# Scaling attention probabilities on VectorE, regrouping the gated unit, and splitting late norm chunks from PSUM

## The reference

```
# gated unit: D_FF = 2816 = 22 chunks of 128
up = hn @ w_up
gate = gelu(causal_dwconv(up[..., :D_FF], conv_f_w, conv_f_b))      # 3 taps
h = h + (gate * up[..., D_FF:]) @ w_down
# three norms whose result feeds the next product: cross attention, gated unit, final
y = x * rsqrt(mean(x * x) + 1e-6) * g
# NSA: the selected and the window branch, per head
p = masked_softmax(q k^T)            # here both branches see every earlier token
o = g0 * o_cmp + g1 * (p_sel @ v_sel) + g2 * (p_win @ v_win)        # g: sigmoid gates
```

## Time and profile before

| | us |
|---|---|
| median of 3 runs | 1995.47 |
| lowest, highest | 1994.6, 1995.6 |
| profiled execution, its time | 1993.29 |
| profiled execution, its span | 1991.5 |

### The profile page before, as it was taken

One profiled execution on the slowest core, in us unless ns is written; L12 is line 12 of the kernel. 1 busy time (PEld: TensorE's weight loads), 2 busy tenths in 40 slices (PEclk: granted clock), 3 DMA queues, 4 the chain that ended last, 5 costly groups with the idle time before them and its releaser, 6 DMA issues.

```text
span 1991.5 us, 24447 instructions
## 1 busy us (share of the span) xinstructions
PE 1903.8 (96%) x8906; PEld 1518.8 (76%) x8906; DVE 798.9 (40%) x1245; ACT 422.5 (21%) x827; POOL 1147.5 (58%) x686
## 2 busy tenths in 40 slices
PE   7989999999999999988989999998999989999996
PEld 5868787888888877865778888887765768888885
DVE  4965443453341464646451212126243362112126
ACT  4323312210010020145140101013233231101022
POOL 5635662675666675467546655664642446666652
PEclk9989999999999999989999999999999999999999
DMA  5312331232333335200223332332321123333321
GB/s 221 111 56 83 97 105 42 85 106 85 112 99 95 95 96 201 64 22 1 75 65 104 95 95 84 95 104 70 102 74 32 53 74 96 105 105 96 98 91 43
DMA packets 46879, 175.99 MB, mean 88 GB/s; under 512 B 5200, under 2 KB 5328, under 8 KB 46032
## 3 DMA queue, kind: packets, MB, share of 16 engines
q1 hardware_dynamic: 46512, 169.55, 26.9%
q10 hardware_dynamic: 288, 5.31, 0.7%
HBM read 172.74 MB, written 2.10 MB: 88 GB/s over the span
## 4 chain that ended last, share of the span: by engine, by line
PE 91%; DVE 3%; POOL 3%; issue 1%; ACT 1%; DMA 0%; SPq 0%; POOLq 0%; DVEq 0%; ACTq 0%
PE acc L466 16%; PE acc L468 16%; PE acc L467 16%; PE acc L489 8%; PE acc L490 7%; PE acc L493 7%; POOL p_n L2329 2%; PE acc L1015 1%; PE misc L1048 1%; PE acc L514 1%; PE acc L516 1%; PE acc L515 1%; PE acc L1017 1%; PE acc L1016 1%; PE misc L730 1%
## 5 line engine op out<-in xcount | busy, mean ns | idle before, releaser
L2316 POOL TENSOR_SCALAR w_hi<-raw 128x1024 fp32r<-128x1024 f32 x309 | 336.2, 1088 | 759.3 <-PE acc L493 381.3
L2318 POOL TENSOR_TENSOR w_lo<-raw,w_hi 128x1024 fp32r<-128x1024 f32 x309 | 746.5, 2416 | 25.8
L466 PE MATMUL acc<-x_hi,w_hi 128*128 128x512 f32 x872 | 342.9, 393 | 0.0
L468 PE MATMUL acc<-x_hi,w_lo 128*128 128x512 f32 x872 | 339.6, 389 | 0.0
L467 PE MATMUL acc<-x_lo,w_hi 128*128 128x512 f32 x872 | 339.4, 389 | 0.0
L466 PE MATMUL acc<-y_hi,w_hi 128*128 128x512 f32 x590 | 231.1, 392 | 0.0
L468 PE MATMUL acc<-y_hi,w_lo 128*128 128x512 f32 x590 | 229.6, 389 | 0.0
L467 PE MATMUL acc<-y_lo,w_hi 128*128 128x512 f32 x590 | 229.6, 389 | 0.0
L1718 DVE TENSOR_TENSOR h<-acc,h 128x512 f32<-128x512 f32 x120 | 82.8, 690 | 349.5 <-PE acc L468 215.8
L468 PEld LDWEIGHTS acc<-x_hi,w_lo 128*128 128x128 f32 x872 | 163.7, 188 | 34.1
L466 PEld LDWEIGHTS acc<-x_hi,w_hi 128*128 128x128 f32 x872 | 163.9, 188 | 32.9 <-issue 0.3
(11 more groups left out here) (374 smaller groups left out, 2657.9 us busy)
## 6 DMA issues: line engine op xcount, KB each, us to landing
raw<-weights_dram SPq DMA_DIRECT2D x309, 512.0 KB, 3.5
w_cmp<-w_cmp_dram ACTq DMA_DIRECT2D x1, 4096.0 KB, 15.9
h<-x_dram SPq DMA_DIRECT2D x2, 1024.0 KB, 6.1
out_dram<-h SPq DMA_DIRECT2D x8, 256.0 KB, 2.0
small<-small_dram SPq DMA_DIRECT2D x1, 1408.0 KB, 16.0
small<-small_dram ACTq DMA_DIRECT2D x1, 1088.0 KB, 6.3
mem_in<-mem_dram SPq DMA_DIRECT2D x1, 1024.0 KB, 13.0
const<-const_dram SPq DMA_DIRECT2D x1, 640.0 KB, 9.0
```

The lines of the kernel that those rows point to most:

```text
L466: mm(out, m["w_hi"][:, slot, k], hi[:, k], start=k == 0, stop=False)
L468: last = mm(out, m["w_lo"][:, slot, k], hi[:, k], start=False, stop=k == kc - 1)
L2316: nc.gpsimd.tensor_scalar(hi, m["raw"][:, slot], 1.0, 0.0, ALU.mult, ALU.add).then_inc(sem("weights_high"), 1)
L2318: nc.gpsimd.tensor_tensor(m["w_lo"][:, slot].rearrange("p k n -> p (k n)"), m["raw"][:, slot], bf(hi), ALU.subtract).then_inc(sem("weights ...
```

## The change

- The groups of the gated unit are 7, 7 and 8 chunks, all three written out on VectorE and ScalarE.
- The late opening goes tile by tile: claim the first tile, then its chunks 0 to 6, each after the wait for its low part; so the second and third; then the last chunk for all three. The sum of squares comes after the second tile. The number of products is the same.
- In the three late norms ScalarE writes the scaled chunk to a PSUM bank (`late_bank`: misc 0 or 3 in turn) and `x_hi` from there; VectorE subtracts `x_hi` from the PSUM bank.
- VectorE scales the probabilities (`n_scale`, `tensor_scalar` in place); GpSimd has no part in the attention and runs one loop over all tiles. `p_n`, `n_neg` and `n_sum` have three buffers.
- PE's order is turn(b), scores(b + 3), values(b - 1); ScalarE's is exponentials(b + 2), copy(b); VectorE's is copy(b), scale(b + 1), max(b + 3), pooling step.

```diff
-GLU_GROUPS = [8, 8, 6]
+GLU_GROUPS = [7, 7, 8]
-          ("glu0", 24), ("glu1", 24), ("glu2", 20),
+          ("glu0", 22), ("glu1", 22), ("glu2", 24),
...
+    def late_bank(self, k):
+        return self.misc[:, 3 * (k % 2)]
...
     def late_opening(t0, first_tile, norm):
-        def sums(k):
-            if k == HALF:
+        slots = [(first_tile + j) % RING for j in range(3)]
+        before = chunks_before(norm)
+        for j in range(3):
+            slot = slots[j]
+            claim(t0 + j)
+            for k in range(KC - 1):
+                pe.wait_ge(sem("norm_ready"), before + k + 1)
+                mm(acc[:, slot], m["w_hi"][:, slot, k], x_hi[:, k], start=k == 0, stop=False)
+                mm(acc[:, slot], m["w_hi"][:, slot, k], x_lo[:, k], start=False, stop=False)
+                mm(acc[:, slot], m["w_lo"][:, slot, k], x_hi[:, k], start=False, stop=False)
+            if j == 1:
                 sum_squares(norm)
-        opening_of(t0, first_tile, x_hi, x_lo, "norm_high", "norm_ready", chunks_before(norm), also=sums)
+        pe.wait_ge(sem("norm_ready"), before + KC)
+        for slot in slots:
+            mm(acc[:, slot], m["w_hi"][:, slot, KC - 1], x_hi[:, KC - 1], start=False, stop=False)
+            mm(acc[:, slot], m["w_hi"][:, slot, KC - 1], x_lo[:, KC - 1], start=False, stop=False)
+            mm(acc[:, slot], m["w_lo"][:, slot, KC - 1], x_hi[:, KC - 1], start=False, stop=True).then_inc(sem("tile_done"), 1)
...
+    n_scores(2)
     for b in range(len(BATCHES)):
-        if b + 2 < len(BATCHES):
-            n_scores(b + 2)
         n_turn(b)
+        if b + 3 < len(BATCHES):
+            n_scores(b + 3)
         if b:
             n_values(b - 1)
...  # ScalarE, late norms
-            f(m["x_hi"][:, k], m["h"][:, k], ACT.Copy, scale=pr.col(gain, k)).then_inc(sem("norm_high"), 1)
+            if k >= 2:
+                act.wait_ge(sem("norm_ready"), chunks_before(name) + k - 1)
+            own.link(f(pr.late_bank(k), m["h"][:, k], ACT.Copy, scale=pr.col(gain, k)))
+            f(m["x_hi"][:, k], pr.late_bank(k), ACT.Copy).then_inc(sem("norm_high"), 1)
...  # ScalarE, exponentials
-        if b >= 2:
-            act.wait_ge(sem("n_turned"), 2 * b - 2)
+        if b >= 3:
+            act.wait_ge(sem("n_turned"), 2 * b - 4)
...  # VectorE, late norms
-            v.scalar_tensor_tensor(m["x_lo"][:, k], h[:, k], pr.col(gain, k), bf(m["x_hi"][:, k]), ALU.mult, ALU.subtract)\
-                .then_inc(sem("norm_ready"), 1)
+            v.tensor_tensor(m["x_lo"][:, k], pr.late_bank(k), bf(m["x_hi"][:, k]), ALU.subtract).then_inc(sem("norm_ready"), 1)
...  # VectorE, attention
-    def n_weight(b):
+    def n_scale(b):
         dve.wait_ge(sem("n_exp"), b + 1)
         r = m["n_r"][:, b % 2, :, 0:heads]
-        own.link(v.reciprocal(r, m["n_sum"][:, b % 2, :, 0:heads]))
-        v.tensor_tensor(r, r, gates[:, tb, :, c0:c0 + heads, 1 + br], ALU.mult).then_inc(sem("n_weight"), 1)
+        own.link(v.reciprocal(r, m["n_sum"][:, b % 3, :, 0:heads]))
+        own.link(v.tensor_tensor(r, r, gates[:, tb, :, c0:c0 + heads, 1 + br], ALU.mult))
+        for g in range(2):
+            for i in range(heads):
+                prob = m["p_n"][:, b % 3, g, i * n:(i + 1) * n]
+                last = v.tensor_scalar(prob, prob, r[:, g, i:i + 1], None, ALU.mult)
+            last.then_inc(sem("n_scaled"), 1)
...
```

More of the change, by code:

```diff
@@ L1468, in scalar_program @@
         n = heads * (tb + 1) * P
+        if b + 2 < len(BATCHES):
+            n_exp(b + 2)
         act.wait_ge(sem("n_turned"), 2 * b + 1)
@@ L1976, in vector_program, with glu_group @@
     conv_bias = pr.view("conv_f_b")
-    def glu_group(g, t0, n, step, norm=None):
-        def scalar(view, j):
-            if isinstance(g, int):
-                return view[:, 8 * g + j:8 * g + j + 1]
-            return view[:, j:j + 9][:, bass.ds(g * 8, 1)]
-        for j in range(n):
+    def glu_group(g):
+        t0, before = START["glu%d" % g], sum(GLU_GROUPS[:g])
+        for j in range(GLU_GROUPS[g]):
             t = t0 + 2 * j
-            gate, up = (acc[:, (START["glu0"] + 2 * j + i) % RING] for i in range(2))
+            gate, up = acc[:, t % RING], acc[:, (t + 1) % RING]
@@ L1987, in glu_group @@
             src = m["g_in"][:, j % 2]
+            w = [conv_w[:, x, before + j:before + j + 1] for x in range(CONV_F)]
             dve.wait_ge(sem("tile_done"), t + 1)
-            step.link(v.tensor_tensor(src[:, CONV_F - 1:], gate, m["r_late"], ALU.mult))
-            step.link(v.tensor_scalar(gate, src[:, 0:S], scalar(conv_w[:, 0], j), scalar(conv_bias, j),
-                                      ALU.mult, ALU.add))
-            step.link(v.scalar_tensor_tensor(gate, src[:, 1:S + 1], scalar(conv_w[:, 1], j), gate, ALU.mult, ALU.add))
@@ L1993, in glu_group @@
-            v.scalar_tensor_tensor(gate, src[:, 2:S + 2], scalar(conv_w[:, 2], j), gate, ALU.mult, ALU.add)\
-                .then_inc(sem("glu_conv"), 1)
+            own.link(v.tensor_tensor(src[:, CONV_F - 1:], gate, m["r_late"], ALU.mult))
+            own.link(v.tensor_scalar(gate, src[:, 0:S], w[0], conv_bias[:, before + j:before + j + 1], ALU.mult, ALU.add))
+            own.link(v.scalar_tensor_tensor(gate, src[:, 1:S + 1], w[1], gate, ALU.mult, ALU.add))
+            v.scalar_tensor_tensor(gate, src[:, 2:S + 2], w[2], gate, ALU.mult, ALU.add).then_inc(sem("glu_conv"), 1)
@@ L2002, in glu_group, with glu_take @@
             dve.sem_inc(sem("tile_out"), 1)
-        def add(c):
-            take(t0 + 2 * n + c, (START["glu0"] + 2 * n + c) % RING, c)
-        if norm:
-            residual_rms(norm, add, "final_g")
-        else:
-            for c in range(KC):
-                add(c)
-    with dve.Fori(0, 2) as g:
-        glu_group(g, g * 24 + START["glu0"], 8, Own(dve, sem("glu_step"), g * 32))
-    glu_group(2, START["glu2"], 6, Own(dve, sem("glu_tail_step")), "fin")
+    def glu_take(g, c):
+        t = START["glu%d" % g] + 2 * GLU_GROUPS[g] + c
+        take(t, t % RING, c)
@@ L2018, in vector_program @@
+    for g in range(2):
+        glu_group(g)
+        for c in range(KC):
+            glu_take(g, c)
+    glu_group(2)
+    residual_rms("fin", lambda c: glu_take(2, c))
     t0 = START["nsa_in"]
@@ L2319, in split @@
                                 ALU.subtract).then_inc(sem("weights_split"), 1)
-    def n_scale(b):
-        tb, br, c0, heads = BATCHES[b]
-        n = (tb + 1) * P
-        pool.wait_ge(sem("n_weight"), b + 1)
-        for g in range(2):
-            for i in range(heads):
-                prob = m["p_n"][:, b % 2, g, i * n:(i + 1) * n]
-                last = nc.gpsimd.tensor_scalar(prob, prob, m["n_r"][:, b % 2, g, i:i + 1], None, ALU.mult)
-            last.then_inc(sem("n_scaled"), 1)
-    ahead = START["nsa_out"] // RING
     for slot in range(RING):
         split(slot, slot, 1)
-    with pool.Fori(1, ahead) as r:
-        for slot in range(RING):
-            split(slot, r * RING + slot, r + 1)
-    for slot in range(RING - 1):
-        split(slot, ahead * RING + slot, ahead + 1)
-    for b in range(len(BATCHES)):
-        n_scale(b)
-    split(RING - 1, ahead * RING + RING - 1, ahead + 1)
-    with pool.Fori(ahead + 1, N_TILES // RING) as r:
+    with pool.Fori(1, N_TILES // RING) as r:
         for slot in range(RING):
```

74 lines of the change are left out of this document (37 added, 37 removed).

## The result

| | before | after |
|---|---|---|
| median, us | 1995.03 (4 runs) | 1971.23 (4 runs) |
| lowest, highest | 1994.35, 1995.6 | 1970.17, 1973.02 |
| profiled execution: time, span | 1993.29, 1991.5 | 1971.24, 1969.4 |
| mean granted clock | 0.984 | 0.987 |

The ratio after to before is 0.9884, 95% interval [0.9872, 0.9897]: faster by 23.8 us of the medians and 22.1 us of the two spans. The forecast was 1976.1, a gain of 19.4.

What follows compares the result with a forecast made beforehand. PE, busy 1903.8 of 1991.5 us, was taken as the bound; only its waits or lower clock give time back. Gains 8.9 + 10.5 = 19.4 us off 1993.29 give 1973.9, plus 2.2 to the median: 1976.1, range 1970.5 to 1987.5.

Steps and rivals of the forecast that it cites:

- The wait for the split: Last gated group: PE's 7.43 us wait for GpSimd's split goes, plus 1.5 us of lower clock; 8.9 us, between 6.9 and 9.1.
- Low parts from PSUM at zero: Three late norms: VectorE's faster low parts buy no PE time, as PE waits for none; zero, bounds 0 to +1.3 us each.
- The attention's term: Attention stage: scaling on VectorE with scores three ahead gains 10.5 us, from a loss of 2.4 to a gain of 14.
- the one-block sum: Two one-block attention batches: VectorE's work plus 1.5 us for the lower clock gives 10.0 us instead of 13.3, gain 3.3.
- The steps of the scalings: Attention: VectorE's scalings take steps of 0.20, 0.27, 0.34 and 0.40 us for 128, 256, 384 and 512 columns; 19.4 us in all.
- The third buffer and the three-ahead order: Attention: the third probability buffer lets exponentials go before the transposes of the batch before are done; scores run three ahead.
- the ring: Attention hand-overs from scores to transposes two batches later: about 6.1 us for two passes, 3.1 each, under PE's 3.38.
- B: Attention: hand-overs take half of the gain, as in-order queues shift the wait to VectorE; 1981.5 us, chance 0.13.
- C: Attention: VectorE scales at one column per cycle, twice the assumed steps, a loss of 2.4 us; 1989 us, chance 0.06.
- D: Late openings stall on the first tile's chunks, 3 x 1.3 = 4 us lost; 1980 us, chance 0.05.
- E: Attention: GpSimd's splits lock out VectorE's scales, 2.3 us at a time; slower, twelve meetings would give 2004 us; chance 0.03.
- the two upper bounds: Largest gains allowed: 14 us in the attention, if the lower clock goes too, and 9.1 us at the split wait.

Runs made afterwards that it cites:

- u6: Changed kernel with the old opening (three tiles claimed at once) and low parts from SBUF; groups 7, 7, 8 and the attention edits stay: 1972.58 us.
- u1: Changed kernel with groups 8, 8, 6 again; the new late opening, the split from PSUM and the attention edits stay: 1971.51 us.
- u3: Changed kernel with groups 8, 8, 6 and low parts from SBUF again; of the late-norm edits only the tile-by-tile opening stays: 1970.9 us.
- u5: Changed kernel with groups 8, 8, 6, old opening and low parts from SBUF again; only the attention edits stay: 1980.29 us.
- x4: Changed kernel with the old two-ahead attention order and two probability buffers; VectorE still scales: 1969.44 us.
- x2: Changed kernel with every probability scaling issued twice on VectorE, once into an unused buffer: 1985.6 us, stage 101.4 us.
- x1: Changed kernel with one GpSimd addition of 1024 columns per attention batch, into an unused buffer: 2006.56 us, stage 122.4 us.
- u4: Changed kernel with groups 8, 8, 6 and the old opening again; of the late-norm edits only the split from PSUM stays: 1977.09 us.
- w1: Changed kernel with the old two-ahead attention order; VectorE still scales, with three probability buffers: 1969.14 us.

## Why the prediction came out right, step by step

- **The wait for the split: right in size, incomplete in cause.** 7.43 us went, and the three edits are worth 9.1 against 8.9. The prediction asked for both parts (longer tiles, later claim) so that "nothing stays". Each alone is enough (u6, u1, u3). The 9.1 stands at the upper bound of the term, and the opening's 17.2 us came as computed. With the opening alone PE asks at 742.5 us only for the first of the three tiles, the fifth of the seven splits. In u3 that one begins at 737.69 and is done at 741.7, and PE opens at 742.52 without a wait. Five splits at 3.96 us against 20.4 us of products is the sum that should have stood there. With the groups alone (u6) no wait is left either, where the prediction's 27.7 against 27.2 us allowed 0.5: not every split meets a low part, and the seven take 27.0.
- **Low parts from PSUM at zero: right here, but not for the reason given.** They last 0.68 us, as forecast. That the faster form frees GpSimd, 0.46 us a tile, was left out. With the wait gone it is worth nothing.
- **The attention's term, 10.5 us, was too small.** After's profile gives 11.3, and u5, where nothing else is changed, 12.5 by its stage, 13.2 by the profiled executions and 14.6 by the medians. By parts, forecast and measured in after: ahead of the first turned batch 7.6 and 7.4; one-block batches 10.0 and 13.5; two-block 15.6 and 13.8; three-block 25.4 and 24.9; four-block with what follows 30.0 and 28.1. The step that failed is the one-block sum, 3.5 us off in after and 2.2 in u1, where the clock was at the lower level for less time: I added up DVE's work and left out that ScalarE's copy is queued behind exponentials that wait for DVE. The other parts were costed too high: each two-block pass takes 3.45 against 3.7 plus a share of a low part, and the four-block part is 1.5 us, not 3, above eight passes of 3.33. The errors of opposite sign hid each other; the sum is closer than its parts by luck.
- **The steps of the scalings: right.** 0.20, 0.27, 0.34 and 0.40 were estimated from one row. In after, 8 of 128 columns take 1.66 us, thus (1.66 - 0.28) / 7 = 0.20; 2 of 512 take 0.88, thus 0.40. With DVE full in the three-block batches (3.11 us a pass, 3.17 forecast) and PE in the four-block ones (3.33, 3.38 forecast), the bound changes engine where the prediction has it. But 3.38 is not what PE needs: in the old order it does the same pass in 3.18.
- **The third buffer and the three-ahead order: wrong.** The prediction held that the buffer "is what lets the exponentials go" and that the ring is shorter by it. x4 has neither and its stage is 1.9 us shorter at like clock. What shortened the ring is GpSimd's 3.1 us leaving it. The passes of before, too, were misread: GpSimd's scalings of four-block batches began 3.38 to 4.43 us apart, not 3.4 to 3.8.
- **The rivals.** B did not come: the hand-overs cost 3.5 us in one place, not half of the gain. C has its total right, its parts off by up to 3 us (x2), and its premise wrong (484 ns at 512 columns, where 0.7 us and more would have borne it out). Its sum also leaves out the 1.5 us of lower clock that the forecast's own sum has. D did not come: the late openings have no wait. E's mechanism is real (x1: 1.6 us of stage per GpSimd operation, where 2.3 was taken), and absent because GpSimd has one split to do in the stage.
- **What no term held.** The time at 1.2 GHz differs between executions without a change in the instructions. The one-block part of after had a mean clock of 0.75, that of u1, whose attention is the same, 0.86; the other parts of the two agree within 0.01 us. The row of u1:

```profile
854.80:866.97 12.17, 8.56 (x63) 5.38 (x61) 10.68 (x28) 7.38 (x30) 0.00 (x0) 0.86 0.01 1
```

Both traces have their wait of 3.48 us in this part. The missing share of the clock, times the length of the part, doubled, is the time at the lower level: 0.25 x 13.54 x 2 = 6.8 us in after, 0.14 x 12.17 x 2 = 3.4 in u1, and 0.38 x 13.31 x 2 = 10.1 before. PE ran at half speed for 3.4 us more in after than in u1, and its stage is 1.4 us longer (87.7 against 86.3). So one-block parts, and stages, are comparable only at like clock. Of the 11.3 us that the attention gained in after's profile up to 1.7 are such clock, of u5's 12.5 (clock 0.86 too) up to 3.4: half of the time at 1.2 GHz that went, estimates from these rows, and too high where PE was idle.
- **Where the miss of 4.4 us by medians stands.** 4.1 of it is in the attention's term (14.6 by u5's median against 10.5), 0.2 in the late norms' (9.1 against 8.9), and 0.1 is the difference of two medians of before (1995.03 and 1994.93). But 1.5 of the 14.6 is no gain of the attention: the profiled execution of before, from which the rows come, was 1.6 us faster than the median beside u5 (1993.29 against 1994.93), while u5's own was 0.2 from its median. The slower executions of before have the lower mean clock (0.983 at 1995.21 us, 0.986 at 1992.77). Where the 0.6 us lies that the profiled executions gained outside the stage stays open.
- **The range: hit with little left.** The gain of 23.8 us lies above the two upper bounds together, 14 + 9.1; the measured 1971.23 is inside 1970.5 to 1987.5 only because the range was widened beyond them.

## What to carry to other kernels

Where several edits aim at one wait, cost each alone: the second cure is worth nothing, and the sum must not need both. For a stage of small batches, sum the busiest engine per pass, and then follow the first passes instruction by instruction through each in-order queue; the first wait lay there and no sum of busy times shows it. An order that helps one placement of the work can close a ring with another: test order and placement apart, compare single profiles part by part and only at like clock, and keep GpSimd's work away from VectorE's scalings in SBUF, and from its operations with two SBUF inputs, where these are on the path.

## What the runs showed of the hardware

- A two-column multiplication with two SBUF inputs, 0.16 us by itself, lasted 1.62 and 1.80 us beside GpSimd's add, to the end of the add (x1). What matters is not how long the operation is but what it meets.
- The blocking works both ways: GpSimd's `w_hi` lasts 1.50 us instead of 1.06 while DVE makes low parts from two SBUF operands (u3), and 1.06 while it makes them from PSUM (u4).
- 22 GpSimd operations of 2.38 us, 52.3 us of work on an otherwise idle engine, lengthened the stage by 34.7 us (122.4 against 87.7).
- The same PE products took 3.18 us per four-block pass in one written order and 3.33 in the other, at full clock and without a wait of PE (w1, after).
